# A two-block transformer layer on one core: the second experts' weight ring begun one stage earlier, an eighth slot for the first experts, matmuls that write nothing used, and a final norm taken tile by tile

## The reference, cut to what matters

```python
def _ec_moe(h, w_router, w_eg, w_eu, w_ed):            # first block's experts
    aff = jax.nn.softmax((h @ w_router).astype(jnp.float32), axis=-1)
    gate, idx = lax.top_k(jnp.transpose(aff, (0, 2, 1)), cap)          # cap = 64 tokens of 512
    xg = h[b_idx, idx]
    hid = jax.nn.silu(jnp.einsum('becd,edf->becf', xg, w_eg)) * jnp.einsum('becd,edf->becf', xg, w_eu)
    yo = jnp.einsum('becf,efd->becd', hid, w_ed) * gate[..., None].astype(h.dtype)
    return jnp.zeros_like(h).at[b_idx, idx].add(yo)

def second_block(...):
        merged = gate_rw * (y_rw @ w_branch_rw[l]) + gate_mla * (y_mla @ w_branch_mla[l])
        x = x + merged @ w_out[l]                       # the output projection
        h2 = rmsnorm(x, ffn_norm_g[l])
        x = x + hier_moe(h2, ...)                       # 32 experts: (silu(x w_g) * (x w_u)) w_down
    return rmsnorm(x, final_norm_g)
```

## Time and profile before

| | us |
|---|---|
| median of 3 runs | 3594.27 (3591.18 to 3597.16) |
| the profiled execution, its time | 3598.31 |
| its span in the trace | 3596.5 |
| TensorE matmul busy | 3148.0 (88%) |
| VectorE busy | 1070.2 (30%) |
| ScalarE busy | 558.9 (16%) |
| matmul groups of the first experts, L1992 and L2026 | 456.7 and 238.8 |
| matmul groups of the second experts, L3677 and L3696 | 121.3 and 64.3 |

### The profile page before, as it was taken

The page is one execution under the profiler, slowest core; times in us unless marked ns, Lnnn a source line. Parts: engine busy times, 40 slices in busy tenths (PEclk is TensorE's granted clock), DMA queues, the critical chain, the costliest instruction groups (busy, mean ns, idle before and its releaser), DMA issues. The chain is left out here.

```text
span 3596.5 us, 37828 instructions
## 1 busy us (share of the span) xinstructions
PE 3148.0 (88%) x15792; PEld 1667.6 (46%) x15792; DVE 1070.2 (30%) x2063; ACT 558.9 (16%) x1178; POOL 286.4 (8%) x270
## 2 busy tenths in 40 slices
PE   6997889998899999698999999987996789995984
PEld 5444645664554444453344434433545763643331
DVE  2233702454573301410111011103056553522112
ACT  2002510112452200100000000002022221301111
POOL 0003000002761000000000000000002200001000
PEclk9998998998899999699999999998998999996997
DMA  7721021110001222379999999996310021017996
GB/s 264 257 71 47 2 74 35 47 36 0 24 1 47 94 70 70 164 295 428 424 425 428 424 424 412 421 423 277 128 35 2 3 109 49 12 59 275 404 425 259
DMA packets 132079, 669.33 MB, mean 186 GB/s; under 512 B 17578, under 2 KB 45645, under 8 KB 98889
## 3 DMA queue, kind: packets, MB, share of 16 engines
q1 hardware_dynamic: 115385, 630.24, 43.5%
q10 hardware_dynamic: 11488, 28.31, 2.1%
q0 software_dynamic: 5040, 8.40, 0.7%
HBM read 672.15 MB, written 14.69 MB: 191 GB/s over the span
## 5 line engine op out<-in xcount | busy, mean ns | idle before, releaser
L1992 PE MATMUL ec_wide<-ec_ring,ec_xg 128*64 128x512 f32 x2048 | 456.7, 600 | 20.8 <-issue 15.4
L1992 PEld LDWEIGHTS ec_wide<-ec_ring,ec_xg 128*64 128x64 f32 x2048 | 148.1, 138 | 309.3 <-issue 305.1
L2026 PE MATMUL ec_acc<-ec_ring,ec_hidT 128*64 128x512 f32 x1024 | 238.8, 622 | 36.4 <-DMA ec_ring<-in_w_exp_down 34.5
L2151 DVE TENSOR_SCALAR ec_xg<-ec_piece,ordered 128x128 f32<-128x128 f32 x64 | 21.9, 405 | 579.7 <-PE ec_piece L2040 579.7
L2026 PEld LDWEIGHTS ec_acc<-ec_ring,ec_hidT 128*64 128x64 f32 x1024 | 84.9, 143 | 188.1 <-issue 188.1
L3677 PE MATMUL hm_gu<-hm_ring,hm_xg 128*64 128x512 f32 x512 | 121.3, 629 | 15.8 <-DMA hm_ring<-in_moe_w_gu,hm_again_rows 7.7
L2040 PEld LDWEIGHTS ec_piece<-ec_sel,x 128*128 128x128 f32 x512 | 122.9, 336 | 8.6 <-issue 5.7
L2040 PE MATMUL ec_piece<-ec_sel,x 128*128 128x128 f32 x512 | 124.4, 406 | 2.8 <-DVE ec_sel L2133 2.8
L2727 POOL TENSOR_TENSOR solve_T<-const_rw,solve_T 128x512 f32<-128x512 f32 x8 | 10.1, 1266 | 1321.3 <-DVE solve_T L2765 1321.3
L2115 ACT ACTIVATE ec_hidT<-ec_acc 128x512 f32<-128x512 f32 x32 | 17.4, 594 | 516.1 <-PE ec_acc L2015 516.1
L1141 PE MATMUL conv_main<-hT,conv_early 128*128 128x512 f32 x192 | 86.2, 605 | 1.6 <-DVE bcT L1217 1.6
(11 more groups left out here) (624 smaller groups left out, 4957.3 us busy)
## 6 DMA issues: line engine op xcount, KB each, us to landing
ec_ring<-in_w_exp_gate SPq DMA_DIRECT2D x64, 2048.0 KB, 13.6
ec_ring<-in_w_exp_up SPq DMA_DIRECT2D x64, 2048.0 KB, 22.2
ec_ring<-in_w_exp_down SPq DMA_DIRECT2D x64, 2048.0 KB, 17.3
hm_ring<-in_moe_w_gu SPq DMA_DIRECT2D x32, 2048.0 KB, 27.3
hm_ring<-in_moe_w_down SPq DMA_DIRECT2D x16, 2048.0 KB, 29.1
ahead_qkv<-in_w_in SPq DMA_DIRECT2D x10, 2048.0 KB, 9.6
key<-in_w_ada ACTq DMA_DIRECT2D x4, 2048.0 KB, 8.7
v<-in_w_ada ACTq DMA_DIRECT2D x4, 2048.0 KB, 10.2
```

The lines of the kernel that those rows point to most:

```text
L1992: last = pe.matmul(wide[half(e), b, :], xg[:, u % 2, j, half(e)], w[e][:, a, b * 512:(b + 1) * 512], start=(j == 0), stop=(j == KD - 1))
L2026: last = pe.matmul(acc[half(e), h, :], hidT[:, f, half(e)], w[e][:, r, h * 512:(h + 1) * 512], start=(f == 0), stop=(f == FT - 1))
```

## The change

Six edits:

1. `EC_SLOTS` goes from 7 to 8.
2. The ring of the second experts is allocated before `p_out2`. Its slots 0 to 6 (`HM_HEAD`) are loaded by SP during `p_out2`; slot 7 is allocated and loaded in `route_experts`; slot 8 is the tile `u2T` itself, loaded in `route_experts` after `p_out2` has read it. The store of the normalised rows comes behind them. The second mixer's body is only moved out of one `with` block.
3. `keep_clocked` issues matmuls whose result nobody reads: 12 behind the scores of the first routing, 72 behind L2255.
4. 12 more of them in `fine_experts`, behind `lists(1)`.
5. The final norm takes each tile's root by itself, and VectorE starts on a tile as soon as its root is there.
6. ScalarE's table for the root is loaded at the start of the final norm.

```diff
+def keep_clocked(k, pe, bank, n):
+
+    for _ in range(n):
+        pe.matmul(bank[:, 0:P], k.const("ones"), k.const("ident"), start=True, stop=True)
...
-EC_SLOTS = 7
+EC_SLOTS = 8
...
+HM_HEAD = HM_SLOTS - 2
...
-        self.tile = scope.enter_context(k.nc.sbuf_tensor("hm_ring", [P, HM_SLOTS, PIECE], F32))
-        self.rows = scope.enter_context(k.nc.sbuf_tensor("hm_again_rows", [P, 2 * LT], mybir.dt.uint32))
+        self.head = scope.enter_context(k.nc.sbuf_tensor("hm_ring", [P, HM_HEAD, PIECE], F32))
+        self.places = [self.head[:, n, :] for n in range(HM_HEAD)] + [None, last]
...
+    def complete(self, scope):
+        self.places[HM_HEAD] = scope.enter_context(self.k.nc.sbuf_tensor("hm_ring_late", [P, PIECE], F32))[:, :]
+        self.rows = scope.enter_context(self.k.nc.sbuf_tensor("hm_again_rows", [P, 2 * LT], mybir.dt.uint32))
...
             norm.turn(pe, scores)
+            keep_clocked(k, pe, norm.pt[:, 0, :], 12)
             pe.wait_ge(aff_ready, 1)
             for t in range(LT):
                 last = pe.transpose(wide[0:E, t * P:(t + 1) * P], aff[:, t, :], k.const("ident"))
             last.then_inc(wide_ready, 1)
+            keep_clocked(k, pe, norm.pt[:, 0, :], 72)
             pe.wait_ge(chosen_T, 1)
...
-            project_rows_onto(k, "p_out2", k.dram["w_out_2"][0], KD, uT, k.residual, 2, ahead)
+    k.rounds_ring = RoundsRing(k, k.second_scope, uT[:, :, :].rearrange("p j n -> p (j n)"))
+    project_rows_onto(k, "p_out2", k.dram["w_out_2"][0], KD, uT, k.residual, 2, ahead,
+                      also=lambda sp: k.rounds_ring.load_first(sp, range(HM_HEAD)))
...
-            ring.load_first(sp, range(3))
+            ring.load_first(sp, range(HM_HEAD, HM_SLOTS))
             sp.wait_ge(norm.row_ready, LT)
             sp.dma_start(xn_rows.rearrange("(t p) d -> p t d", p=P), norm.xn[:, :, :]).then_inc(xn_stored, 16)
-            ring.load_first(sp, range(3, HM_SLOTS))
...
             lists(0)
             lists(1)
+            pe.wait_ge(index_ready, 2)
+            keep_clocked(k, pe, list_, 12)
             flips(0)
...
+            act.preload_act_table(ACT.Sqrt)
             for t in range(LT):
                 link(act.activation(square[:, :], x[:, t, :], ACT.Square, accum_out=ss[:, t:t + 1]))
-            act.activation(rstd[:, :], ss[:, :], ACT.Sqrt, scale=1.0 / D, bias=k.const("eps")).then_inc(root_ready, 1)
+                act.activation(rstd[:, t:t + 1], ss[:, t:t + 1], ACT.Sqrt, scale=1.0 / D, bias=k.const("eps")).then_inc(root_ready, 1)
...
-            dve.wait_ge(root_ready, 1)
             dve.wait_ge(loaded, 16)
-            link(dve.reciprocal(rstd[:, :], rstd[:, :]))
             for t in range(LT):
+                dve.wait_ge(root_ready, t + 1)
+                link(dve.reciprocal(rstd[:, t:t + 1], rstd[:, t:t + 1]))
                 dve.scalar_tensor_tensor(y[:, t, :], x[:, t, :], rstd[:, t:t + 1], gain[:, :], ALU.mult, ALU.mult).then_inc(row_ready, 1)
```

More of the change, by code:

```diff
@@ L1608, in branch, with project_rows_onto @@
     project(k, label + "_b", w, feats, width, D // width, groups, merge, link_steps=1 if add else 0, ahead=ahead, then=then)
-def project_rows_onto(k, label, w, kt, xT, residual, n_chunks, ahead):
+def project_rows_onto(k, label, w, kt, xT, residual, n_chunks, ahead, also=None):
     x = residual.tile
@@ L1623, in wait_loaded @@
         dve.wait_ge(residual.loaded, 16)
-    project(k, label, w, kt, 512, n_chunks, groups, add, ahead=ahead, first=wait_loaded)
+    project(k, label, w, kt, 512, n_chunks, groups, add, ahead=ahead, first=wait_loaded, also=also)
 def project_rows(k, label, w, kt, xT, out, n_chunks, width=512, ahead=None, then=None, also=None):
@@ L1871, with __init__ @@
 class RoundsRing:
-    def __init__(self, k, scope):
+    def __init__(self, k, scope, last):
         self.k = k
@@ L1883, in __init__ @@
         self.index = {job: n for n, job in enumerate(self.order)}
-        self.tile = scope.enter_context(k.nc.sbuf_tensor("hm_ring", [P, HM_SLOTS, PIECE], F32))
-        self.rows = scope.enter_context(k.nc.sbuf_tensor("hm_again_rows", [P, 2 * LT], mybir.dt.uint32))
+        self.head = scope.enter_context(k.nc.sbuf_tensor("hm_ring", [P, HM_HEAD, PIECE], F32))
+        self.places = [self.head[:, n, :] for n in range(HM_HEAD)] + [None, last]
         self.first_loaded = [k.semaphore(f"hm_first_loaded{n}") for n in range(HM_SLOTS)]
         scope.callback(lambda: k.clear(self.first_loaded))
+    def complete(self, scope):
+        self.places[HM_HEAD] = scope.enter_context(self.k.nc.sbuf_tensor("hm_ring_late", [P, PIECE], F32))[:, :]
+        self.rows = scope.enter_context(self.k.nc.sbuf_tensor("hm_again_rows", [P, 2 * LT], mybir.dt.uint32))
     def load_first(self, sp, slots):
         for n in slots:
-            sp.dma_start(*second_weights(self.k, self.tile[:, n, :], *self.order[n])).then_inc(self.first_loaded[n], 16)
+            sp.dma_start(*second_weights(self.k, self.places[n], *self.order[n])).then_inc(self.first_loaded[n], 16)
     def enter(self, sem):
@@ L1899, in load_again @@
         if kind == "gu":
-            parts = [(self.tile[:, n, :], self.k.dram["moe_w_gu_2"][0].rearrange("e (p a) n -> (e p) (a n)", p=P), 2 * u + e)]
+            parts = [(self.places[n], self.k.dram["moe_w_gu_2"][0].rearrange("e (p a) n -> (e p) (a n)", p=P), 2 * u + e)]
         else:
-            parts = [(self.tile[:, n, i * PIECE // 2:(i + 1) * PIECE // 2], self.k.dram["moe_w_down_2"][0].rearrange("e (p f) n -> (e p) (f n)", p=P), 2 * u + i)
+            parts = [(self.places[n][:, i * PIECE // 2:(i + 1) * PIECE // 2], self.k.dram["moe_w_down_2"][0].rearrange("e (p f) n -> (e p) (f n)", p=P), 2 * u + i)
                      for i in range(2)]
@@ L1912, in load @@
     def load(self, sp, n):
-        sp.dma_start(*second_weights(self.k, self.tile[:, n % HM_SLOTS, :], *self.order[n])).then_inc(self.loaded[n % HM_SLOTS], 16)
+        sp.dma_start(*second_weights(self.k, self.places[n % HM_SLOTS], *self.order[n])).then_inc(self.loaded[n % HM_SLOTS], 16)
     def wait(self, pe, *job):
@@ L1921, in wait @@
             pe.wait_ge(self.loaded[n % HM_SLOTS], 16 * (n // HM_SLOTS))
-        return self.tile[:, n % HM_SLOTS, :]
+        return self.places[n % HM_SLOTS]
 def stream_experts(k, ring, x, rstd, rank, gate, scale_cols, shift_cols, out):
@@ L3450, in route_experts @@
+    k.rounds_ring = RoundsRing(k, k.second_scope, uT[:, :, :].rearrange("p j n -> p (j n)"))
+    project_rows_onto(k, "p_out2", k.dram["w_out_2"][0], KD, uT, k.residual, 2, ahead,
+                      also=lambda sp: k.rounds_ring.load_first(sp, range(HM_HEAD)))
+    late.close()
+    low.close()
 def route_experts(k, norm, scale, constants, ring, rank, place, first, share, rounds, xn_rows, ordered):
@@ L3606, in fine_experts @@
         BACK = 2 * LT
-        back = ring.tile[:, 0:BACK * D // PIECE, :].rearrange("p s (b n) -> p (s b) n", n=D)
+        back = ring.head[:, 0:BACK * D // PIECE, :].rearrange("p s (b n) -> p (s b) n", n=D)
         gu, turn, acc, flip, list_ = ps("gu", [P, 2, 512]), ps("turn", [P, 512]), ps("acc", [P, 2, 512]), ps("flip", [P, 2, 512]), ps("list", [P, 512])
@@ L3836, in second_experts @@
         out = k.residual.tile
-        with ExitStack() as s:
-            ring = RoundsRing(k, s)
+        with k.second_scope as s:
+            ring = k.rounds_ring
+            ring.complete(s)
             ordered = tile(s, "hm_ordered", [P, KD])
@@ L3873, in two_blocks @@
         k.ordered = tile(everything, "ordered", [P, 2, KD])
-        k.branch_scope = ExitStack()
+        k.branch_scope, k.second_scope = ExitStack(), ExitStack()
         first_mixer(k, dram["x"])
```

179 lines of the change are left out of this document (88 added, 91 removed).

## The result

The changed kernel took **3569.57 us** (median of 4 runs, 3568.54 to 3572.14) against 3593.66 of the kernel before in the same session (3591.18 to 3597.16): ratio 0.9933, 95% interval 0.9916 to 0.9951, or 24.1 us less. The forecast was 3575.4, 18.9 less, in a range of 3563 to 3588.

The account below looks back on a forecast made before the run. Both expert stages were taken to be bound by their DMA bytes. The terms -9.9 + 4.9 - 12.0 - 1.9 = -18.9 us, from the median of 3594.27, gave 3575.4 us, range 3563 to 3588.

Parts of the forecast that it names:

- What bounds the kernel: Both expert stages end when their bytes have come, with DMA share 1.00 and 1.01 at 422 GB/s.
- The eighth slot, -9.9: First experts' weight ring: one piece less to load, 4.9 us, and fewer dips in DMA rate, 5 us.
- between 0 and 9.5 I take half: First experts: dips cost 9.5 us; one more load in flight fills 5 us, as TensorE has 34.5 us of waits.
- First routing, +4.9: Unused matmuls there: 12 delay L2255 by 3.7 us, 72 delay the marks' transposes by 3.5, faster counts return 2.3.
- The second ring, -12.0: Second experts' start: early loads leave DMA engines idle, so `hidden(0)` starts 10.0 us earlier and runs 2.0 us shorter.
- what was costed at nothing: Seven loads within `p_out2` and the later store of rows: no cost; failure would show as waits or a late first fetch.
- Final norm, -1.9: End of kernel: table first and a root per tile let VectorE end at 3590.1 instead of 3592.03 us.
- The unused matmuls at 0.22 whatever the clock: Rival, first routing: 0.22 to 0.243 us a record, routing about +23, end 3593, no change; 10%.
- load and matmul in series at 0.44: Slower rival: each weight load waits for the matmul before it, +59 in the first routing, end 3637; 4%.
- The third, empty loads slow by themselves: Rival, second experts' start: empty indirect loads take 12.6 us whatever the traffic, -2.4 replaces -12.0, end 3585; 9%.
- The sum: All four terms together: -18.9 us, taken from the median of 3594.27.

Follow-up runs that it names:

- the two experiments: Changed kernel with EC_SLOTS back at 7: 3583.98 us, ratio 0.997; kernel before with only EC_SLOTS = 8: 3579.8 us, ratio 0.9957.
- its experiment: Changed kernel with the old final norm (one root for all four tiles, table loaded behind the squares, one reciprocal): 3570.75 us, ratio 0.9927.
- the last kernel: Changed kernel with five edits to unused matmuls and final norm loads, then three more to the second routing, first flips and first fetch: 3556.14 us, ratio 0.9883.

## Why the prediction was right, point by point

**What bounds the kernel.** Right. Both expert stages end with their bytes: an earlier first reload moved the end by as much (the second stage's reload is 23.1 us earlier in the trace, the final block 24.1), and fewer bytes or dips shortened them.

**The eighth slot, -9.9.** The mechanism was right; the size was wrong, in the term "between 0 and 9.5 I take half". It measured -13.4 between the traces, -11.9 in that of the kernel before with eight slots, and -13 and -15.5 by the ratios of the two experiments. The piece is 4.9, so of the -13.4 the dips gave 8.5, of the 9.5 that I had counted. The trace of before held what was needed to see it: the gather's 15.55 us and a `hidden` of 7 behind it, during which no slot comes free, are 4.6 pieces of 4.9 us, and one slot more closes just such a gap. The reason that I gave for a half, waits that TensorE has to give, says nothing of the dips.

**First routing, +4.9.** Measured +2.8. The dozen delayed L2267 by 2.7 and not 3.7, since the clock rose inside it, and 24 records took 4.58 us and not 5.3 (5.10 in the trace with seven slots, where it rose later). The 72 delayed the marks by 2.2 and not 3.5, since a record is 0.113 and not 0.117 and the transposes in front took 0.60 in place of 1.02. The counts gave 2.2 (2.3 forecast). A further 0.2 stands between the first gate matmuls and the first reload.

**The second ring, -12.0.** Measured -13.8 at the final block and -12.8 at the first reload: `hidden(0)` came 10.4 us earlier (10.0 forecast) and was 2.4 shorter (2.0). The order in it was other than I wrote: the empty loads took 2.1 us on idle engines and not 4.7, so they no longer decide; the dozen does, 1.5 us behind the rows, and `hm_xg`. I left out that lists and flips between `hidden(0)` and `hidden(1)` also run at 2.4 GHz (5.0 us in place of 6.1), and that the clock falls again before `hidden(1)`, which takes 8.59. Whether that makes the last 1.0 us is not shown, since the stretch behind the first reload varied by more than 2 us with the same code. Nothing of what was costed at nothing appeared: no wait for `ahead` in the output projection, and the rows were there.

**Final norm, -1.9.** Measured -2.1 between the traces, -1.8 by its experiment. The gain took 4.2 us and not 3.5, a tile 1.4 and not 1.5. The table took its 1.28 us and the first square began right behind it, so the drain that the Trainium skill adds (ScalarE: Activation LUTs, What ACT_TABLE_LOAD costs) did not show here either.

**The rivals.** The unused matmuls at 0.22 whatever the clock, and load and matmul in series at 0.44, both fall by the 144 records in 16.24 us. The Trainium skill's rule for the second (TensorE: Matmul & The Clock Gate, The mechanism), that a load overlaps only where the row group differs, did not hold for these: 144 loads filled 16.16 us while the matmuls ran. The same section also lets a load go ahead into a background weight buffer; no run here shows which of the two the chip did. The third, empty loads slow by themselves, falls by 2.1 us.

**The sum.** The traces differ by 7.3 us more than the sum forecast (26.2 against 18.9): the eighth slot 3.5, the routing 2.1, the second ring 1.8, the norm 0.2, all in one direction, so no error covered another. In the medians it is 5.2 us more (24.1 against 18.9) and not 7.3, since the profiled execution of before was further above its median than that of after.

## What to carry to other kernels

Size a weight ring by the longest stretch in which the consumer frees no slot, divided by the time of one load: here 22.5 us by 4.9. The slot that crosses it was worth about three times its own piece; that the next one brings little is judged from the dips that are left, not run. Work that fills the engines' queues belongs in a stage where they idle, since small indirect transfers behind full queues took 10 us or more here in place of 2 to 4. Unused matmuls pay where real ones on the path follow at once: 3.0 us in `hidden(0)`, 2.1 in the counts. Their number must fit the idle time of the engine to the last one: 72 where 48 fit cost 2.2 us, and a dozen where the engine was idle for 1.6 us cost 2.7.

## What the runs showed of the hardware

- Unused matmuls with the same weights, 128 columns loaded and 128 moving, took 0.113 us a record, its load included, at 2.4 GHz (144 in 16.24) and 0.23 at 1.2 GHz (24 in 5.49), while the gather's matmuls of the same shape took 0.243 at both clocks (15.55 us for 64, whether the clock rose inside, as at 1531.07, or was 1.00 throughout, as in later gathers). Their weights are read with a stride of eight floats; that this is the reason was not tried.
- Twice the granted clock fell under matmuls with few columns moving. In the last kernel 28 records of 32 columns began at 2.4 GHz at 3253.95, and the mean clock of 3256 to 3258 was 0.69, so it fell at about 3256.8, with TensorE busy and the last eight still running (0.92 us of idle time lay before them). In the changed kernel it fell at the end of the 20 records of 16 columns, to 0.50 from about 1528.
- An indirect load whose row numbers are all out of bounds, and which moves nothing, still took 2.1 us from issue to landing on idle DMA engines (median of four) and 12.6 beside full queues (median of seven).
